# Two transformer-like blocks on one core: more seven-product slots in the second feed-forward products, and three of four of their weight sums made during the first products, kept in DRAM and loaded

## The chip, the cores and the metric

The kernel runs on 1 core of one Trainium2 chip. The metric is the device time of a launch in microseconds (us). The kernel before took a median of 2221.39 us over 3 runs (2220.28 to 2221.83).

## The reference

Two blocks on 256 tokens of width 2048 in fp32, one after the other. Each has a mixer (block 1: neighbourhood attention, a state-space mixer and memory attention; block 2: four kinds of attention) and a feed-forward part. What matters here is the feed-forward part, width 8192, twice in the program:

```python
h = rmsnorm(x, norm_mlp_pre[l])
f = jnp.square(jax.nn.relu(h @ w_ff1[l])) @ w_ff2[l]     # block 1; block 2: w_up, w_down
x = x + rmsnorm(f, norm_mlp_post[l])
```

## The kernel before

**Precision.** Products of fp32 matrices are made of three matmuls on rounded parts: high x high, high x low, low x high. For each weight tile ScalarE writes the rounded high part and VectorE the low part (tile minus high). TensorE can only start on a slot when both have passed over it.

**Slots.** Weights come through a ring of 4 slots of 1 MB (128 partitions x 2048 floats, `raw_weights`), loaded by the queue of SyncE (SP): it waits on `split_ready` until VectorE has split the slot four earlier, then asks for the next load. High and low parts (`w_high`, `w_low`) have two buffers each. Every engine walks the slots in the order in which the program writes them out, and engines meet by semaphores.

**Ups.** `up` makes the hidden layer (`ff1_1` of block 1, `ff1_2` of block 2): 8 iterations of 8 slots. A slot is 16 wide matmuls (512 columns) and 16 narrow ones (256). After slots 0 and 4 of an iteration ScalarE and VectorE move a finished group out of PSUM (`evac_hidden`, `summed`, `squared`). The order on VectorE is `low(0)`, `low(1)`, `summed`, `squared`, `low(2)` and so on, where `low(j)` splits slot j.

**Downs.** `down` multiplies the hidden layer by the second weights (`ff2_1`, `ff2_2`): two passes h = 0, 1 over the left and right 1024 output columns, each 32 slots r of 2 x 128 rows. A **plain slot** is 4 banks x 2 row tiles x 3 = 24 matmuls of 512 columns (lines 841 to 843). A **seven-product slot** (the list `SUMMED`, 11 of the 32) takes its 2 x 2 blocks of weights W0..W3 and of activations by Strassen's scheme in Winograd's form: 7 block products instead of 8, so 21 matmuls (lines 856 to 858). For this it needs sums. `sums(h, r)` on VectorE makes, in this order, s1 and s3 of x, the weight sums t1 and t3 (W1 + W0, W2 + W0; 128 x 1024, L2603), s2, t2 = W2 + t1 (L2607), s4, and t4 = W3 + t2, which overwrites W0 in the ring (L2611). Then ScalarE rounds and VectorE splits: the four plain blocks as `quad_high` and `quad_low` (L1709, L2619), the sums of x (L2617, L2621) and t1, t3, t2 (L2623, L2625). All these have one buffer. ScalarE rounds `quad_high` when TensorE has done the first four products of the seven-product slot before (`quad_used`), and the other sums when it has done that slot (`split_used`).

**The order on VectorE.** `down` goes over r: first `sums` of slot r + 1 if that is a seven-product slot, then the split of slot r itself. The first sums of a pass stand ahead of slot 0, those of slot 2 of the first pass in a scratch of their own. In the first pass `last_summed` and `last_squared` of the up stand behind slots 0 and 1. Four `keep` steps stand about slot 0 of the second pass, and `combine` (the seven products' banks into `home`) ahead of slot 30. In the last pass of `ff2_2` there are also two left halves (L2390), ahead of slots 29 and 30, and two `ahead` steps (L2397), ahead of slot 31. TensorE there does banks 0 to 2 of slots 30 and 31 before bank 3 of both.

GpSimd has no part in the ups and downs, and issues no DMA.

## Time and profile before

| | |
|---|---|
| median of 3 runs | 2221.39 us |
| the profiled execution, span | 2219.3 us |
| TensorE busy | 2195.5 us, 99% |
| VectorE busy | 1613.8 us, 73% |
| ScalarE busy | 1163.2 us, 52% |
| GpSimd busy | 93.2 us, 4% |
| DMA, mean rate | 181 GB/s |
| granted TensorE clock, mean | 0.999 |
| first up, first down | about 426 to 785 us, 785 to 1119 us |
| second up, second down | about 1510 to 1873 us, 1873 to 2206 us |

A timeline row has the start, the length, the engine, the line, the operation, its output and inputs, and in brackets the idle time before it with what ended it. Lengths of neighbouring operations overlap, since an engine starts one while the last drains: the price of an operation is the distance between two starts. A row with x2 holds two operations merged.

### The profile page before, as it was taken

How to read it: one execution, taken by the hardware profiler on the slowest of the kernel's cores; microseconds unless marked ns; L12 is line 12 of the kernel's file. 1: busy time of each engine (PE TensorE's matmuls, PEld its weight loads, DVE VectorE, ACT ScalarE, POOL GpSimd, SP SyncE). 2: the span in 40 equal slices, each digit the busy share in tenths (PEclk: the TensorE clock that was granted, in tenths of full speed). 3: DMA queues.
4: the chain of work that ended last, by engine and by line, in shares of the span. 5: the costliest groups of instructions: out<-in, count | busy, mean ns of one | idle time of the engine just before them, and what ended most of it. 6: DMA issues, size and time to landing. Idle time of an engine off the chain costs nothing.

```text
span 2219.3 us, 32872 instructions
## 1 busy us (share of the span) xinstructions
PE 2195.5 (99%) x13128; PEld 1892.6 (85%) x13128; DVE 1613.8 (73%) x2013; ACT 1163.2 (52%) x1682; POOL 93.2 (4%) x66
## 2 busy tenths in 40 slices
PE   8999999999999999999999999999999999999998
PEld 7888988888888888888898988888888888888886
DVE  7878565665454599899886578847454547998997
ACT  6433465543443466566664466646434345665665
POOL 0553000000000000000000000000000000000000
PEclk9999999999999999999999999999999999999999
DMA  8364445555556666667654533455565565666663
GB/s 328 121 153 161 151 134 211 168 190 189 189 188 188 187 194 207 195 205 258 199 166 144 172 115 98 136 196 163 187 189 189 189 189 173 215 201 195 209 202 114
DMA packets 169923, 402.65 MB, mean 181 GB/s; under 512 B 15296, under 2 KB 30912, under 8 KB 165968
## 3 DMA queue, kind: packets, MB, share of 16 engines
q1 hardware_dynamic: 158496, 394.83, 55.3%
q10 hardware_dynamic: 11312, 6.22, 1.2%
q8 instruction: 80, 1.31, 0.2%
q14 instruction: 35, 0.29, 0.0%
HBM read 398.90 MB, written 2.13 MB: 181 GB/s over the span
## 4 chain that ended last, share of the span: by engine, by line
PE 94%; DVE 4%; ACT 1%; issue 1%; DMA 0%; SPq 0%; DVEq 0%; ACTq 0%
PE ps L768 21%; PE ps L773 11%; PE ps L841 7%; PE ps L842 6%; PE ps L843 6%; PE ps L657 5%; PE ps L857 3%; PE ps L856 3%; PE ps L858 3%; PE ps L665 3%; PE ps L666 3%; PE ps L667 3%; PE ps L1075 2%; PE ps L1077 2%; PE ps L1076 2%; PE ps L679 2%
## 5 line engine op out<-in xcount | busy, mean ns | idle before, releaser
L2497 DVE TENSOR_TENSOR w_low<-raw_weights,w_high 128x1024 fp32r<-128x1024 f32 (+1 forms) x403 | 474.3, 1215 | 422.1 <-ACT w_high L1574 418.3
L1574 ACT ACTIVATE w_high<-raw_weights 128x1024 fp32r<-128x1024 f32 (+1 forms) x378 | 377.4, 1046 | 408.0 <-PE ps L773 279.8
L768 PE MATMUL ps<-x_split,w_high 128*128 128x512 f32 x2048 | 494.1, 391 | 1.7 <-DVE x_split L2485 1.7
L768 PEld LDWEIGHTS ps<-x_split,w_high 128*128 128x128 f32 x2048 | 374.6, 188 | 74.2 <-issue 3.0
L773 PEld LDWEIGHTS ps<-x_split,w_low 128*128 128x128 f32 x2048 | 265.8, 191 | 12.1
L773 PE MATMUL ps<-x_split,w_low 128*128 128x256 f32 x2048 | 269.4, 283 | 0.0
L841 PE MATMUL ps<-w_high,x_split 128*128 128x512 f32 x672 | 262.0, 390 | 0.5 <-issue 0.4
L842 PE MATMUL ps<-w_low,x_split 128*128 128x512 f32 x672 | 261.5, 389 | 0.0
L843 PE MATMUL ps<-w_high,x_split 128*128 128x512 f32 x672 | 261.4, 389 | 0.0
L2582 DVE TENSOR_TENSOR w_low<-raw_weights,w_high 128x1024 fp32r<-128x1024 f32 x168 | 197.8, 1219 | 1.7 <-ACT w_high L1689 1.6
L1689 ACT ACTIVATE w_high<-raw_weights 128x1024 fp32r<-128x1024 f32 x168 | 167.6, 1045 | 0.0
L666 PE MATMUL ps<-x_split,w_high 128*128 128x256 f32 x544 | 153.8, 283 | 0.0
L841 PEld LDWEIGHTS ps<-w_high,x_split 128*128 128x128 f32 x672 | 126.1, 188 | 29.0 <-issue 3.0
L843 PEld LDWEIGHTS ps<-w_high,x_split 128*128 128x128 f32 x672 | 126.1, 188 | 26.3
L842 PEld LDWEIGHTS ps<-w_low,x_split 128*128 128x128 f32 x672 | 126.2, 188 | 25.7
L665 PE MATMUL ps<-x_split,w_high 128*128 128x256 f32 x416 | 121.4, 292 | 0.8 <-DVE x_split L2485 0.4
L667 PE MATMUL ps<-x_split,w_low 128*128 128x256 f32 x416 | 117.5, 282 | 0.0
L657 PE MATMUL ps<-x_over_high,raw_weights 128*128 128x256 f32 x512 | 115.0, 382 | 0.0
L1709 ACT ACTIVATE x_split<-raw_weights 128x1024 fp32r<-128x1024 f32 x88 | 88.1, 1048 | 47.1 <-DVE raw_weights L2611 47.1
L2619 DVE TENSOR_TENSOR x_split<-raw_weights,x_split 128x2048 fp32r<-128x2048 f32 x44 | 100.7, 2288 | 16.2 <-ACT x_split L1709 16.2
L657 PEld LDWEIGHTS ps<-x_over_high,raw_weights 128*128 128x128 f32 x512 | 95.9, 190 | 14.6 <-issue 1.2
L666 PEld LDWEIGHTS ps<-x_split,w_high 128*128 128x128 f32 x544 | 104.2, 191 | 0.2
(376 smaller groups left out, 3657.9 us busy)
## 6 DMA issues: line engine op xcount, KB each, us to landing
raw_weights<-in_w_ff SPq DMA_DIRECT2D x128, 1024.0 KB, 5.4
raw_weights<-in_w_up SPq DMA_DIRECT2D x64, 1024.0 KB, 5.2
raw_weights<-in_w_down SPq DMA_DIRECT2D x64, 1024.0 KB, 5.5
raw_weights<-in_w_in SPq DMA_DIRECT2D x62, 1024.0 KB, 5.3
raw_weights<-in_w_out SPq DMA_DIRECT2D x32, 1024.0 KB, 4.9
raw_weights<-in_w_mem_kv SPq DMA_DIRECT2D x7, 1024.0 KB, 14.6
residual<-in_xT SPq DMA_DIRECT2D x2, 2048.0 KB, 13.9
region<-t_table ACTq DMA_DIRECT2D x1, 3072.0 KB, 18.9
```

The lines of the kernel that those rows point to most:

```text
L657: last = nc.tensor.matmul(acc[:, c], w[:, P * c:P * c + P], x, start=(kt == 0 and c % 2 == 0), stop=(kt == kts - 1), skip_group_check=True)
L665: nc.tensor.matmul(o, h, xh_, start=(first and c % 2 == 0), stop=False, skip_group_check=True)
L666: nc.tensor.matmul(o, h, xl_, start=False, stop=False, skip_group_check=True)
L667: last = nc.tensor.matmul(o, wl[:, P * c:P * c + P], xh_, start=False, stop=done, skip_group_check=True)
L768: nc.tensor.matmul(hidden_ps(g)[:, c], w[:, P * c:P * c + P], xs[:, kt], start=(kt == 0), stop=False, skip_group_check=True)
L773: last = nc.tensor.matmul(hidden_ps(g)[:, c, 0:S], w[:, P * c:P * c + P], xh[:, kt], start=False, stop=(kt == KT - 1), skip_group_check=True)
L841: nc.tensor.matmul(o, x_high[:, x], wh[:, c], start=(r == 0 and q == 0), stop=False, skip_group_check=True)
L842: nc.tensor.matmul(o, x_high[:, x], wl[:, c], start=False, stop=False, skip_group_check=True)
L843: last = nc.tensor.matmul(o, x_low[:, x], wh[:, c], start=False, stop=True, skip_group_check=True)
L1574: nc.scalar.activation(split_slot(wh_t, k)[:, r], ring_slot(n)[:, r], ACT.Copy).then_inc(rounded, 1)
L2497: V.tensor_tensor(split_slot(wl_t, k)[:, r], ring_slot(n)[:, r], split_slot(wh_t, k)[:, r].bitcast(f32), ALU.subtract).then_inc(split_read ...
L2582: V.tensor_tensor(split_slot(wl_t, k)[:, w], ring_slot(n)[:, w], split_slot(wh_t, k)[:, w].bitcast(f32), ALU.subtract).then_inc(split_read ...
```

## The change

Seven-product slots are now 2, 4, ... 28, so 14 a pass instead of 11. Counted through both passes of a down (0 to 27), all but every fourth (3, 7, ... 27) are **staged**: 21 a down. During the up before it, GpSimd loads the 1 MB of weights of such a slot into a free tile (`mix_t` or `xres_t`), VectorE makes t1, t3, t2 and t4 in three additions after slots 0, 3 and 6 of each iteration but the first, and GpSimd stores the four sums as a record in DRAM, with the load of the next record beside it. In the down SP loads t1, t3 and t2 straight to where ScalarE rounds them, and t4 in the place of W0, beside W1 and W2, W3, into the ring slot, by three DMAs; `sums` makes only the sums of x. The first record's load waits for `t5_masked` in `ff1_1` and for `residual_row` 1 in `ff1_2`. SP's queue in the down is unrolled, and at its slot 4 waits for the last record and the end of the up. The sums of slot 2 now stand between slots 0 and 1 in both passes, and `combine` ahead of slot 31. On ScalarE `first_product` moves one slot later as well. The diff, cut to its core:

```diff
+        w_sums = nc.dram_tensor("weight_sums", (28, P, 2048), f32, kind="Internal").ap()
...
-        sums_at = [(rinv, place("sums", 22528, 1024)), (region[:, 16384:17408], region[:, 17408:18432])]
+        sums_a, sums_b = rinv, place("sums", 22528, 1024)
+        stage_of = {"ff1_1": mix_t, "ff1_2": xres_t, "ff2_1": mix_t, "ff2_2": xres_t}
...
-        SUMMED = (2, 5, 7, 10, 12, 15, 17, 20, 22, 25, 27)
+        SUMMED = tuple(range(2, PAIRS - 3, 2))
+        AHEAD_OF = tuple(j for j in range(2 * len(SUMMED)) if j % 4 != 3)
+        RECORDS = len(AHEAD_OF)
+        STAGED = RECORDS // (FF1_ITERS - 1)
+        STAGE0 = {"ff1_1": 0, "ff1_2": RECORDS, "ff2_1": 0, "ff2_2": RECORDS}
...
+        def ahead_count(name, c):
+            return STAGE0[name] + sum(j < c for j in AHEAD_OF)
+        def made_before(name, c):
+            return 6 * (SUMMED0[name] + c) - 3 * ahead_count(name, c)
...
             def down(name, w):
-                for j in range(BODY):
-                    load(rows(w, 0, 1024, 2 * j, 2))
                 n0, k0 = SLOT0[name], SPLIT0[name]
-                for lo, hi, back, c0 in ((1, FF2_ITERS // 2, 0, 0), (FF2_ITERS // 2, FF2_ITERS, DFF, 1024)):
-                    with sp.Fori(lo, hi) as i:
-                        for j in range(BODY):
-                            sp.wait_ge(split_ready, i * (2 * BODY) + 2 * (k0 + j - RING + 1))
-                            src = w[bass.ds(i * (2 * BODY * P) + (2 * P * j - back), 2 * P), c0:c0 + 1024]
-                            sp.dma_start(ring_slot(n0 + j).rearrange("p (k c) -> p k c", k=2),
-                                         src.rearrange("(k p) c -> p k c", p=P)).then_inc(slot_loaded[(n0 + j) % RING], 16)
-                state["n"] = n0 + BODY * FF2_ITERS
+                before = {}
+                for c in AHEAD_OF:
+                    before[4 if c == 0 else slot_before(c - 1, SUMMED) + 4] = c
+                for q in range(2 * PAIRS):
+                    (h, r), n = divmod(q, PAIRS), n0 + q
+                    sp.wait_ge(split_ready, 2 * (k0 + q - RING + 1))
+                    if q == 4:
+                        sp.wait_ge(staged, 32 * (STAGE0[name] + RECORDS))
+                        sp.wait_ge(split_used, k0)
+                    if q in before:
+                        c = before[q]
+                        sp.dma_start(sums_a, w_sums[AHEAD_OF.index(c), :, 0:1024]).then_inc(raws_loaded, 16)
+                        sp.dma_start(sums_b[:, 0:512], w_sums[AHEAD_OF.index(c), :, 1024:1536]).then_inc(raws_loaded, 16)
+                    if r in SUMMED and summed_count(h, r) in AHEAD_OF:
+                        c = summed_count(h, r)
+                        got = rest_loaded[ahead_count(name, c) % 2]
+                        src = w[2 * P * r:2 * P * (r + 1), 1024 * h:1024 * h + 1024].rearrange("(k p) c -> p k c", p=P)
+                        sp.dma_start(ring_slot(n)[:, HALF:SLOT], src[:, 1]).then_inc(slot_loaded[n % RING], 16)
+                        sp.dma_start(ring_slot(n)[:, 512:HALF], src[:, 0, 512:1024]).then_inc(got, 16)
+                        sp.dma_start(ring_slot(n)[:, 0:512], w_sums[AHEAD_OF.index(c), :, 1536:2048]).then_inc(got, 16)
+                    else:
+                        src = w[2 * P * r:2 * P * (r + 1), 1024 * h:1024 * h + 1024].rearrange("(k p) c -> p k c", p=P)
+                        sp.dma_start(ring_slot(n).rearrange("p (k c) -> p k c", k=2), src).then_inc(slot_loaded[n % RING], 16)
+                state["n"] = n0 + 2 * PAIRS
...
                     act.wait_ge(split_used, SPLIT0[name])
+                    act.wait_ge(staged, 32 * (STAGE0[name] + RECORDS))
                 act.wait_ge(gains_loaded, 16)
                 nc.scalar.activation(sh[:, 0:384], pair_of(r, P, 384), ACT.Copy).then_inc(sums_rounded, 1)
                 act.wait_ge(slot_loaded[n % RING], 16 * (n // RING + 1))
-                act.wait_ge(sums_made, 6 * s + 6)
+                if c in AHEAD_OF:
+                    u = ahead_count(name, c)
+                    act.wait_ge(rest_loaded[u % 2], 32 * (u // 2 + 1))
+                else:
+                    act.wait_ge(sums_made, made_before(name, c + 1))
                 for half_ in range(2):
                     a = slice(SLOT // 2 * half_, SLOT // 2 * (half_ + 1))
                     nc.scalar.activation(quad_high[:, a], w[:, a], ACT.Copy).then_inc(rounded, 1)
                 if c:
                     act.wait_ge(split_used, SPLIT0[name] + slot_before(c - 1, SUMMED) + 1)
+                act.wait_ge(sums_made, made_before(name, c + 1))
                 nc.scalar.activation(sh[:, 384:896], sums_b[:, 512:1024], ACT.Copy).then_inc(sums_rounded, 1)
+                if c in AHEAD_OF:
+                    act.wait_ge(raws_loaded, 32 * (ahead_count(name, c) + 1))
                 nc.scalar.activation(th[:, 0:1024], sums_a, ACT.Copy).then_inc(sums_rounded, 1)
...
-                        if r == PAIRS - 3:
+                        if r == PAIRS - 2:
                             first_product(name, h + 1)
...
+            def stage(name, w, free):
+                t = stage_of[name]
+                def store(c):
+                    pool.wait_ge(sums_staged, ADDS * (STAGE0[name] + c + 1))
+                    if c + 1 < RECORDS:
+                        load(c + 1)
+                    pool.dma_start(w_sums[c], t[:, 2048:4096]).then_inc(staged, 16)
+                def load(c):
+                    h, r = AHEAD_OF[c] // len(SUMMED), SUMMED[AHEAD_OF[c] % len(SUMMED)]
+                    src = w[2 * P * r:2 * P * (r + 1), 1024 * h:1024 * h + 1024].rearrange("(k p) c -> p k c", p=P)
+                    pool.dma_start(t[:, 0:2048].rearrange("p (k c) -> p k c", k=2), src).then_inc(staged, 16)
+                free()
+                load(0)
+                for c in range(RECORDS):
+                    store(c)
...
+            stage("ff1_1", A["w_ff2"], lambda: pool.wait_ge(dve_done, at("t5_masked")))
...
+            stage("ff1_2", A["w_down_2"], lambda: pool.wait_ge(act_done, at("residual_row", 1)))
...
+                t = stage_of[name]
+                w, sums_ = (t[:, a:a + 2048].rearrange("p (b c) -> p b c", c=512) for a in (0, 2048))
+                stage_after = {0: 0, 3: 1, 6: 2}
+                def staged_sums(q, i):
+                    c = STAGE0[name] + q - STAGED
+                    dve.wait_ge(staged, i * (32 * STAGED) + (32 * c + 16))
+                    V.tensor_tensor(sums_[:, 0:2], w[:, 1:3], w[:, 0].unsqueeze(1).to_broadcast([P, 2, 512]), ALU.add).then_inc(sums_staged, 1)
+                    dve.wait_ge(sums_staged, i * (3 * STAGED) + (3 * c + 1))
+                    V.tensor_tensor(sums_[:, 2], w[:, 2], sums_[:, 0], ALU.add).then_inc(sums_staged, 1)
+                    dve.wait_ge(sums_staged, i * (3 * STAGED) + (3 * c + 2))
+                    V.tensor_tensor(sums_[:, 3], w[:, 3], sums_[:, 2], ALU.add).then_inc(sums_staged, 1)
                 def body(i, first=False):
                     for j in range(4 if first else 0, BODY):
                         low(name, j, i)
+                        if j in stage_after and not first:
+                            staged_sums(stage_after[j], i)
...
                 def sums(h, r):
-                    n, s = SLOT0[name] + PAIRS * h + r, SUMMED0[name] + summed_count(h, r)
-                    (sums_a, sums_b), w = scratch_of(h, r), ring_slot(n).rearrange("p (b c) -> p b c", c=512)
-                    t1, t2, t13 = sums_a[:, 0:512], sums_b[:, 0:512], sums_a.rearrange("p (b c) -> p b c", c=512)
+                    n, s, c = SLOT0[name] + PAIRS * h + r, SUMMED0[name] + summed_count(h, r), summed_count(h, r)
                     s1, s2, s4 = sums_b[:, 512:640], sums_b[:, 768:896], sums_b[:, 896:1024]
                     s13 = sums_b[:, 512:768].rearrange("p (b c) -> p b c", c=P)
                     x = pair_of(r).rearrange("p (b c) -> p b c", c=P)
                     if h == 0:
                         dve.wait_ge(hidden_ready, HIDDEN_OF[name] + r // 2 + 1)
-                    if (h, r) == (0, SUMMED[0]):
-                        dve.wait_ge(t5_out, 16)
-                    elif (h, r) == (0, SUMMED[1]):
-                        dve.wait_ge(split_used, SPLIT0[name])
-                    c = summed_count(h, r)
                     if c:
                         dve.wait_ge(split_ready, 2 * (SPLIT0[name] + slot_before(c - 1, SUMMED) + 1))
+                    else:
+                        dve.wait_ge(split_used, SPLIT0[name])
                     V.tensor_tensor(s13, x[:, 0:2], x[:, 2::-2], ALU.subtract).then_inc(sums_made, 1)
+                    m0 = made_before(name, c)
+                    if c in AHEAD_OF:
+                        dve.wait_ge(sums_made, m0 + 1)
+                        V.tensor_tensor(s2, s1, x[:, 1], ALU.subtract).then_inc(sums_made, 1)
+                        dve.wait_ge(sums_made, m0 + 2)
+                        V.tensor_tensor(s4, x[:, 3], s2, ALU.add).then_inc(sums_made, 1)
+                        return
...
-                        if r == PAIRS - 2:
+                        if r == PAIRS - 1:
                             combine(name, h + 1)
                         if (h, r) == (1, PAIRS - 1) and ahead is not None:
                             for t in range(TT):
                                 ahead(t)
-                        if r == 0:
-                            sums(h, SUMMED[0])
-                            if h:
-                                keep(name, 0)
-                        elif r + 1 in SUMMED[1:]:
+                        if (h, r) == (1, 0):
+                            keep(name, 0)
+                        if r + 1 in SUMMED:
                             sums(h, r + 1)
                         if r in SUMMED:
                             summed(h, r)
```

## Rows read from the trace of the kernel before

**Rows 1.** The page: the span, and busy time, share and count of each engine.

```profile
span 2219.3 us, 32872 instructions
...
PE 2195.5 (99%) x13128; PEld 1892.6 (85%) x13128; DVE 1613.8 (73%) x2013; ACT 1163.2 (52%) x1682; POOL 93.2 (4%) x66
```

**Rows 2.** Windows, an up, a down: stretch, length, busy time by engine, clock, DMA.

```profile
560.00:700.00 140.00, 140.00 (x805) 123.69 (x805) 72.49 (x63) 56.65 (x57) 0.00 (x0) 1.00 0.59 188
...
850.00:1000.00 150.00, 149.65 (x661) 123.61 (x660) 139.67 (x174) 91.57 (x117) 0.00 (x0) 1.00 0.64 203
```

**Rows 3.** Timeline, TensorE, a down: start, length, engine, line, operation, tiles.

```profile
905.00 0.39 PE L841 MATMUL ps<-w_high,x_split 128*128 128x512 f32 x1
...
915.88 0.39 PE L856 MATMUL ps<-x_split,mem_high 128*128 128x512 f32 x1
...
920.64 0.39 PE L841 MATMUL ps<-w_high,x_split 128*128 128x512 f32 x1
```

**Rows 4.** Timeline, VectorE, a down: six sums, then a plain slot.

```profile
902.89 0.41 DVE L2601 TENSOR_TENSOR sums<-region 128x256 f32<-128x256 f32 x1
...
903.23 1.22 DVE L2603 TENSOR_TENSOR rinv<-raw_weights 128x1024 f32<-128x1024 f32 x1
...
904.36 0.28 DVE L2605 TENSOR_TENSOR sums<-sums,region 128x128 f32<-128x128 f32 x1
...
905.97 0.69 DVE L2578 TENSOR_TENSOR x_split<-region,x_split 128x512 fp32r<-128x512 f32 x1
...
908.84 0.55 DVE L2617 TENSOR_TENSOR mem_high<-region,mem_high 128x384 fp32r<-128x384 f32 x1
```

**Rows 5.** Timeline, ScalarE: it rounds a seven-product slot.

```profile
919.28 1.99 ACT L1709 ACTIVATE x_split<-raw_weights 128x1024 fp32r<-128x1024 f32 x2
```

**Rows 6.** Timeline, VectorE: it splits that slot, and what comes next.

```profile
921.31 2.29 DVE L2619 TENSOR_TENSOR x_split<-raw_weights,x_split 128x2048 fp32r<-128x2048 f32 x1 [0.75 <-ACT x_split L1709]
...
925.86 0.68 DVE L2578 TENSOR_TENSOR x_split<-region,x_split 128x512 fp32r<-128x512 f32 x1
```

**Rows 7.** Timeline, VectorE: the operation behind plain slot 1, first down.

```profile
790.81 1.22 DVE L2544 SCALAR_TENSOR_TENSOR region<-region 128x1024 f32<-128x1024 f32 x1
```

**Rows 8.** Timeline, TensorE: it begins plain slot 1 of the first down.

```profile
791.04 0.47 PE L841 MATMUL ps<-w_high,x_split 128*128 128x512 f32 x1
```

**Rows 9.** Timeline, TensorE: it begins the last slot of the kernel.

```profile
2200.02 0.47 PE L841 MATMUL ps<-w_high,x_split 128*128 128x512 f32 x1
```

**Rows 10.** Timeline, VectorE, the end of the second down.

```profile
2186.80 1.28 DVE L2390 SCALAR_TENSOR_TENSOR region<-region,small_stats,mixed 128x1024 f32<-128x1024 f32 x1
...
2188.88 1.41 DVE L2261 TENSOR_TENSOR region<-region,ps 128x512 f32<-128x512 f32 x2 [0.80 <-ACT region L1723]
...
2194.40 2.60 DVE L2397 SCALAR_TENSOR_TENSOR region<-region,small_stats,mixed 128x1024 f32<-128x1024 f32 x2
...
2197.52 2.35 DVE L2582 TENSOR_TENSOR w_low<-raw_weights,w_high 128x1024 fp32r<-128x1024 f32 x2
```

**Rows 11.** Timeline, VectorE, an up: splits of slots, idle before each.

```profile
625.40 2.36 DVE L2497 TENSOR_TENSOR w_low<-raw_weights,w_high 128x1024 fp32r<-128x1024 f32 x2 [3.20 <-ACT w_high L1574]
...
631.96 2.36 DVE L2497 TENSOR_TENSOR w_low<-raw_weights,w_high 128x1024 fp32r<-128x1024 f32 x2 [4.20 <-ACT w_high L1574]
```

**Rows 12.** Timeline, TensorE, an up: two slots begin.

```profile
629.67 3.82 PE L768 MATMUL ps<-x_split,w_high 128*128 128x512 f32 x16
...
635.24 3.82 PE L768 MATMUL ps<-x_split,w_high 128*128 128x512 f32 x16
```

**Rows 13.** DMA view, 12 to 45 us: packets, rate, many in flight.

```profile
DMA packets 4924, 13.13 MB, mean 398 GB/s; under 512 B 351, under 2 KB 479, under 8 KB 4538
```

**Rows 14.** DMA view, 560 to 700 us: issues, size, median us to landing.

```profile
raw_weights<-in_w_ff SPq DMA_DIRECT2D x25, 1024.0 KB, 5.2
```

**Rows 15.** Timeline, VectorE, first up: the t5 mask, then slot 1.

```profile
468.31 0.68 DVE L2261 TENSOR_TENSOR region<-ps,region 16x512 f32<-16x512 f32 x1 [0.47 <-PE ps L748]
...
476.12 2.36 DVE L2497 TENSOR_TENSOR w_low<-raw_weights,w_high 128x1024 fp32r<-128x1024 f32 x2 [4.86 <-ACT w_high L1574]
```

More of the change, by code:

```diff
@@ L275, in program @@
         out_written = sem("out_written")
+        staged, sums_staged = sem("staged"), sem("sums_staged")
+        rest_loaded, raws_loaded = [sem(f"rest{i}_loaded") for i in range(2)], sem("raw_sums_loaded")
         block = ctx.enter_context(nc.Block())
@@ L479, in pair_of @@
             return hid_f[:, 512 * r + a:512 * r + a + width]
-        def scratch_of(h, r):
-            return sums_at[1 if (h, r) == (0, SUMMED[0]) else 0]
         def ring_slot(n):
@@ L1694, in summed @@
                 s, w = SUMMED0[name] + c, ring_slot(n)
-                sums_a, sums_b = scratch_of(h, r)
                 th, sh = sums_w[name][0], sums_x[name][0]
```

12 lines of the change are left out of this document (7 added, 5 removed).

## The prediction

> **What bounds the kernel now.** I read the page's table of busy times first. TensorE is busy for 99% of the span [rows 1]: a change gains only by taking matmuls away, and loses wherever TensorE is made to wait. The profiled execution took 2219.3 us; the median of the runs is 2221.39, so about 2.1 us lie around the span, and I add the sum of this text to the median. Next, the busy times by stretch [rows 2]: in an up VectorE works 72.5 of 140 us, in a down 139.7 of 150. That share hides the order of the work, so I then read both engines slot by slot. In the down a plain slot is 24 matmuls and a seven-product slot 21, and TensorE goes from slot to slot without a gap [rows 3]: (915.88 - 905.00) / 48 = 0.2267 us for each matmul, 5.44 us for a plain slot, (920.64 - 915.88) = 4.76 for a seven-product slot.
>
> **Term 1, matmuls.** SUMMED grows from 11 to 14 slots in each of four passes: 12 more slots, 3 matmuls fewer in each, 36 x 0.2267 = 8.2 us less. This is certain as work.
>
> **Term 2, the seven-product slot that still makes its own sums (14 times).** On VectorE the six sums take 905.97 - 902.89 = 3.08 us, and the split of a plain slot behind them 908.84 - 905.97 = 2.87 [rows 4]. For a staged slot only the three small sums of x remain, 0.41 + 0.28 + 0.28 with waits between them, about 1.0. So VectorE's total falls, by 42 x 2.1 us. Its place counts more. How soon can VectorE have a seven-product slot ready when the last one but one was also such a slot? The splits have one buffer: ScalarE's rounding waits for TensorE's four first products, VectorE's split of them for the rounding, and the rest for the end of that earlier slot. The trace has this spacing: TensorE ends the earlier slot at 920.64 [rows 3], ScalarE had begun to round at 919.28 [rows 5], VectorE waited for it, split at 921.31 and was free for the next thing at 925.86 [rows 6], 5.2 us after TensorE's end. Before, every such pair was followed by two plain slots, and the six sums of the next one came only after the first of these had been split. After, all seven-product slots stand two apart (2, 4, ... 28), and `sums(h, r + 1)` stands directly ahead of the plain split that TensorE needs next. From TensorE's end of a seven-product slot: 5.2 + 3.08 + 2.87, with about 0.15 for the semaphore, is 11.3; TensorE wants it after one plain and one seven-product slot, at 5.44 + 4.76 = 10.2. It waits 1.1 us. With a staged slot: 5.2 + 1.0 + 2.87 + 0.15 = 9.2, no wait. Of counts 0 to 27 every fourth (3, 7, ... 27) is unstaged, 7 in each down; the one early in the second pass starts with a little less on VectorE (I take 0.9). 2 x (6 x 1.1 + 0.9) = 15 us. The wait cannot be made up: VectorE may not run ahead of the single buffer, however idle it is on average. This term is larger than the gain.
>
> **Term 3, the ends of the downs.** Up to down: VectorE is done with plain slot 1 at 790.81 [rows 7] and TensorE begins it at 791.04 [rows 8], 0.2 us to spare. Before, the first sums were made ahead of slot 0, into a scratch of their own; now about 1.0 us of small sums stands between: 0.8 to 0.9 late, twice, 1.8. First to second pass: the last `keep` ends some 0.9 after TensorE's end of slot 31 (it reads its bank), then 1.0 + 2.87 and the semaphore against 5.44: 0.4 late, twice, 0.8. End of the kernel: after slot 27 VectorE had four plain slots, two left halves, `combine` and two `ahead` steps, and was late for slot 31 by a little (the split of slot 31 runs from 2197.52 to 2199.87 [rows 10] and TensorE begins it at 2200.02 [rows 9]; in step it would have begun some 0.3 earlier). Now slot 28 is a seven-product slot; behind it come 3 x 2.87 for plain slots, 2 x 1.28 for left halves, two pairs of 1.4 for `combine` (about 2.7) and 2.5 for `ahead`, 16.4 us [rows 4, 10], beginning 5.0 us before TensorE's end of it, thus some 11.3 after; TensorE wants slot 31 after 24 + 18 matmuls, 9.5. With the semaphore that is 1.6 to 1.9 late instead of 0.3: 1.4. Together 4.0 us.
>
> **Term 4, the ups.** The three sums per record cost 1.22 [rows 4] + 0.68 + 0.68 (an operation of 128 x 512 [rows 6]) = 2.6 us on VectorE, 42 times, 109 us. They stand where VectorE waits 3.2 us a slot, 4.2 once [rows 11]: hidden, with 0.6 us to spare. TensorE needs 5.57 us a slot (635.24 - 629.67 [rows 12]). What isn't sure is the wait for the record's DMAs, `staged`, with all of VectorE's splits queued behind it, and TensorE behind them. A load and a store of 1 MB go out from GpSimd when the sums are made. The shortest of the three intervals is two slots: 11.1 - 2.6 = 8.5 us until VectorE asks, and TensorE feels it 2.5 later (1.6 that VectorE would idle, 0.9 by which its split is ahead, 634.3 [rows 11] against 635.24 [rows 12]): 11.0. The 16 DMA engines together moved 398 GB/s when all were wanted [rows 13], and one 1 MB load takes 5.2 us to land [rows 14]: 2.6 us are its 1.05 MB at that rate, and 2.6 are fixed. A pair that shares the engines with one ring load: 2.6 + 3 x 2.6 = 10.5, just inside. Over an iteration the need is 14 x 1.05 MB in 44.5 us, 330 GB/s, 83% of the 398. The trace has neither a store of this size nor a GpSimd DMA, so the ends are: 0, and three transfers one behind the other at 5.2, 15.6 - 11.0 = 4.6 us at each of 12 places, 55 us. I take 0, by the nearer row (398 with many in flight), and keep half of the upper end for the range. Nothing below 0: no matmul is removed here. The first load of `ff1_1` goes out only after `t5_masked` (468.31 + 0.68 [rows 15]) and lands 5.2 later, 474.2, or 475.2 with some time for the issue; sums to 477.8, where VectorE went on to slot 1 at 476.12 [rows 15]: 1.7 late against 0.9 of lead, 1 us. In `ff1_2` the load goes out earlier: 0.
>
> The 5.2 us [rows 14] belong to SP's loads. The Trainium skill, "DMA: Bandwidth & Descriptors", section "Issuing engines are not separate DMA queues", says that DMAs issued from GpSimd run on the same 16 engines as those of SP; it speaks against this change, since it gives the stage's traffic no path of its own. Its table of transfers issued from GpSimd has 6.15 us for 1 MB; by that figure a pair in line would take 12.3 and each of the 12 places cost an estimated 1.3 us, 16 us in all. No row here shows such a transfer.
>
> **Edits costed at nothing.** Each staged slot brings 0.75 MB more in the down: 10.75 MB in 40.8 us, 263 GB/s of 398; the raw sums are asked for when the slot before is split and needed some 10 us later, against 5.2. SP waits at slot 4 for the end of the up and for `staged`; queued behind it is slot 4's load, needed three slots (15 us) later. The t5 table (3 MB, second pass of the first down) shares this time: 0 to 3 us. ScalarE's new waits are for landings of the same kind, and it idles beside TensorE. The unrolled SP queue: it only issues.
>
> **Sum.** -8.2 + 15 + 4.0 + 1 = +11.8, and about 1 for the t5 overlap and small delays: 2234.
>
> **Rivals.** (1) The own sums hide after all: TensorE gets its 8.2 us, only terms 3 and half of 4 stay, 2221.4 - 8.2 + 4 = 2217; without term 3 too, 2213. It decides if VectorE is free within 10.2 - 3.08 - 2.87 - 0.15 = 4.1 us of TensorE's end instead of 5.2. For it: VectorE is 93% busy in the down before [rows 2] and would do less, and no wait of this kind stands in the trace; against it: the 5.2 us are a row, and the order is in the code. 0.10. (2) The own sums cost half, 0.5 us each, if VectorE is ready sooner than in the row: 2227. 0.12. (3) The ups wait for `staged`: from a landing later than 11.0 us after the sums each us costs 12; 1 to 2 us (an issue on GpSimd, the receipt of a store) on top of the forecast give 2246 to 2258. For it: a margin of 0.5 us against unmeasured parts. 0.24. (4) The engines saturate below 330 GB/s when loads and stores mix: 14.7 MB at 300 is 48.9 us instead of 44.5, 14 times 4.4, 2296. Loads alone reached 398. 0.05. (5) The change doesn't save what it says: excluded for the matmuls, whose slots are counted in the code. The forecast, 2229 to 2240, has 0.49.
>
> **The range.** Rival 4 and most of rival 1 are left out: 2219 to 2257. A measurement of this kernel can tell 0.2%, 4.4 us, from no change. Faster, below 2217: half of rival 1 and less, 0.06. Within: the rest of it and a part of rival 2, 0.10. Slower: 0.84.
>
> **What the profile of after would show.** 2 x 2 x (18 x 24 + 14 x 21) = 2904 matmuls in the downs, at 0.2267. Waits of TensorE of about 1.1 us before the plain slots 7, 15, 23 of the first passes and 3, 11, 19, 27 of the second, released by VectorE's w_low; none before the plain slots ahead of staged ones. The first plain slot after an up 0.9 late. In the ups, waits of VectorE for `staged` below 2.5 us, and no gap of TensorE; if TensorE has gaps at the second slot of each iteration, rival 3 is right. I'm wrong altogether if VectorE finishes a seven-product slot much sooner than 5.2 us after TensorE's end of the one before.

## The result

The kernel after takes 2245.53 us (median of 4 runs, 2242.28 to 2249.43), the kernel before 2221.61 in the same comparison: a ratio of 1.011, 95% interval 1.0096 to 1.0123. It is 24 us slower, where 12.4 were forecast. Of the runs below, one execution of six of spread_sync took 2415.45 us at a granted clock of 0.849 where the others had 0.998 to 0.999, and is left out of its median.

The profile's page of after: span, then engines with busy time, share and count; below, queues with packets, MB and share of the 16 engines, and two kinds of transfers with count, size and us to landing.

```profile
span 2247.6 us, 33030 instructions
...
PE 2198.2 (98%) x13092; PEld 1890.4 (84%) x13092; DVE 1695.2 (75%) x2109; ACT 1182.4 (53%) x1718; POOL 146.7 (7%) x150
...
q1 hardware_dynamic: 177312, 427.87, 55.9%
q0 software_dynamic: 17472, 88.09, 12.1%
...
mixed<-in_w_ff POOLq DMA_DIRECT2D x21, 1024.0 KB, 7.5
weight_sums<-mixed POOLq DMA_DIRECT2D x21, 1024.0 KB, 9.8
```

Windows of after, an up and a down, with the columns of [rows 2]:

```profile
560.00:700.00 140.00, 137.61 (x786) 121.06 (x786) 94.93 (x89) 55.79 (x56) 11.38 (x18) 1.00 0.94 324
850.00:1000.00 150.00, 146.66 (x644) 120.24 (x643) 131.49 (x163) 94.23 (x124) 0.00 (x0) 1.00 0.73 246
```

Against [rows 1], 36 matmuls are gone, as wanted, yet the span is 28.3 us longer. Against [rows 2], VectorE does less in the down (131.5 us for 139.7), and TensorE loses 3 us there all the same; in the up it loses 2.4, beside transfers at 324 GB/s instead of 188. TensorE's waits in after: engine, line, what it waited for; us in all, times, longest.

```profile
PE ps L868 <- DVE w_low L2654: 20.0, 19, 2.1
...
PE ps L795 <- DVE w_low L2553: 6.6, 5, 2.0
```

Line 868 is the first product of a plain slot, line 795 that of an up's slot. I call a gap what lies between the starts of two matmuls beyond the usual 0.23 us; these are the gaps of after, by kind. **Own sums:** in each down slots 7, 15 and 23 of the first pass begin 1.39 us late, slots 3, 11, 19 and 27 of the second 0.76, 1.27, 1.27, 1.27, one of these 1.27 being 2.26 in the first down: 18.5 us. **Ends:** slot 1 after each up 1.02, slot 1 of each second pass 0.43, the last slot 1.63: 4.5. Before had 0.8 at such places, 0.31 at its last slot and 0.52 at the start of one second pass, so 3.7 are new. **Ups:** 1.94, 1.58, 0.91, 0.34 and 2.04: 6.8. Three stretches of TensorE at half clock, below, cost some 5. With -8.2 for the matmuls the sum is 26; about 2.5 of the profiled 28.3 us I can't place, and this execution was the slowest of the four.

VectorE in after, about slot 7 of the first down, answers [rows 4] and [rows 6]:

```profile
819.10 2.29 DVE L2694 TENSOR_TENSOR x_split<-raw_weights,x_split 128x2048 fp32r<-128x2048 f32 x1 [1.09 <-ACT x_split L1740]
...
823.83 0.42 DVE L2668 TENSOR_TENSOR sums<-region 128x256 f32<-128x256 f32 x1
824.17 1.22 DVE L2679 TENSOR_TENSOR rinv<-raw_weights 128x1024 f32<-128x1024 f32 x1
...
826.92 0.69 DVE L2650 TENSOR_TENSOR x_split<-region,x_split 128x512 fp32r<-128x512 f32 x1
827.52 2.36 DVE L2654 TENSOR_TENSOR w_low<-raw_weights,w_high 128x1024 fp32r<-128x1024 f32 x2
829.79 0.56 DVE L2692 TENSOR_TENSOR mem_high<-region,mem_high 128x384 fp32r<-128x384 f32 x1
```

And TensorE behind it:

```profile
830.02 0.47 PE L868 MATMUL ps<-w_high,x_split 128*128 128x512 f32 x1 [1.23 <-DVE w_low L2654]
```

In step TensorE would have begun at 830.02 - 1.39 = 828.63, so it had ended the seven-product slot before at 818.43. VectorE was free 5.4 us later, the sums took 3.09, the split 2.87, the semaphore 0.23: 11.6 against 10.2. That the 5.4 us come from the single buffer is read from the order in the code and from VectorE's wait for ScalarE (1.09 us at 819.10); no run gives it a second buffer.

### The profile page after: what moved, and what is told of

It reads as the page before. It is cut to its first block, busy times and chain, and to the rows that moved or that the text cites. A ratio compares the mean times of both kernels' runs of the same rounds, so it can differ in the third digit from the quotient of the medians.

```text
span 2247.6 us, 33030 instructions
## 1 busy us (share of the span) xinstructions
PE 2198.2 (98%) x13092; PEld 1890.4 (84%) x13092; DVE 1695.2 (75%) x2109; ACT 1182.4 (53%) x1718; POOL 146.7 (7%) x150
## 4 chain that ended last, share of the span: by engine, by line
PE 77%; DVE 13%; issue 3%; ACT 3%; DMA 3%; POOL 0%; DVEq 0%; SPq 0%; ACTq 0%
PE ps L795 17%; PE ps L800 9%; PE ps L684 5%; PE ps L868 4%; PE ps L869 4%; PE ps L870 4%; PE ps L692 3%; PE ps L693 3%; PE ps L694 3%; PE ps L1102 2%; PE ps L1103 2%; PE ps L1104 2%; DVE w_low L2654 2%; PE ps L885 2%; PE ps L883 2%
## 5 line engine op out<-in xcount | busy, mean ns | idle before, releaser
L868 PE MATMUL ps<-w_high,x_split 128*128 128x512 f32 x576 | 226.5, 393 | 20.0 <-DVE w_low L2654 20.0
L870 PE MATMUL ps<-w_high,x_split 128*128 128x512 f32 x576 | 224.9, 390 | 0.0
L869 PE MATMUL ps<-w_low,x_split 128*128 128x512 f32 x576 | 224.8, 390 | 0.0
L2654 DVE TENSOR_TENSOR w_low<-raw_weights,w_high 128x1024 fp32r<-128x1024 f32 x144 | 169.6, 1220 | 1.5 <-ACT w_high L1716 1.5
L2694 DVE TENSOR_TENSOR x_split<-raw_weights,x_split 128x2048 fp32r<-128x2048 f32 x56 | 128.3, 2292 | 43.0 <-ACT x_split L1740 43.0
L868 PEld LDWEIGHTS ps<-w_high,x_split 128*128 128x128 f32 x576 | 108.5, 188 | 49.5 <-issue 27.4
L1716 ACT ACTIVATE w_high<-raw_weights 128x1024 fp32r<-128x1024 f32 x144 | 143.8, 1047 | 0.0
L870 PEld LDWEIGHTS ps<-w_high,x_split 128*128 128x128 f32 x576 | 108.5, 188 | 22.9
L869 PEld LDWEIGHTS ps<-w_low,x_split 128*128 128x128 f32 x576 | 108.6, 189 | 21.9
L1740 ACT ACTIVATE x_split<-raw_weights 128x1024 fp32r<-128x1024 f32 x112 | 111.7, 1046 | 0.6 <-DVE raw_weights L2687 0.6
```

The costliest lines, as they stand in the source:

```text
L868: nc.tensor.matmul(o, x_high[:, x], wh[:, c], start=(r == 0 and q == 0), stop=False, skip_group_check=True)
L869: nc.tensor.matmul(o, x_high[:, x], wl[:, c], start=False, stop=False, skip_group_check=True)
L870: last = nc.tensor.matmul(o, x_low[:, x], wh[:, c], start=False, stop=True, skip_group_check=True)
L2654: V.tensor_tensor(split_slot(wl_t, k)[:, w], ring_slot(n)[:, w], split_slot(wh_t, k)[:, w].bitcast(f32), ALU.subtract).then_inc(split_read ...
```

## Experiments

All times are medians; before stood at 2220.8 to 2221.0 in these comparisons. **First the two halves of the loss, each by itself.**

**own_out.** The three weight additions of an unstaged slot are left out (its products are then of stale sums).

```diff
-                    V.tensor_tensor(t13, w[:, 1:3], w[:, 0].unsqueeze(1).to_broadcast([P, 2, 512]), ALU.add).then_inc(sums_made, 1)
...
-                    V.tensor_tensor(t2, w[:, 2], t1, ALU.add).then_inc(sums_made, 1)
...
-                    V.tensor_tensor(s4, x[:, 3], s2, ALU.add).then_inc(sums_made, 1)
-                    dve.wait_ge(sums_made, m0 + 4)
-                    V.tensor_tensor(w[:, 0], w[:, 3], t2, ALU.add).then_inc(sums_made, 1)
+                    V.tensor_tensor(s4, x[:, 3], s2, ALU.add).then_inc(sums_made, 4)
```

> The kernel after without the three weight additions of the seven-product slots that are not staged (it leaves out these sums, 14 times in the run, so its products there are wrong; the sums of x stay). If VectorE's own sums ahead of the plain slot's split are what TensorE waits for, the 14 gaps of 1.1 to 1.5 us ahead of plain slots 7, 15, 23 (first half) and 3, 11, 19, 27 (second) go, 18.5 us in all: about 2227 us, against 2245.5 with them. If the ups' transfers or the later loads cost the time, it stays within 3 us of 2245.

Measured 2225.11 us, ratio to before 1.0018 (1.0009 to 1.0027). Additions of 14 x 2.3 = 33 us of VectorE's time are gone (1.14 + 0.60 + 0.60 by the starts in the rows above and around them), and the kernel gains 20.4. No plain slot waits inside a pass any more; the gaps at the ends and in the ups are left, the one at the last slot with 2.12 us instead of 1.63.

**staging_only.** The kernel before, with the staging added to the ups.

```diff
+            stage("ff1_1", A["w_ff2"], lambda: pool.wait_ge(dve_done, at("t5_masked")))
...
+            stage("ff1_2", A["w_down_2"], lambda: pool.wait_ge(act_done, at("residual_row", 1)))
...
                         low(name, j, i)
+                        if j in stage_after and not first:
+                            staged_sums(stage_after[j], i)
```

> The kernel before with the staging of the ups alone: 21 loads, additions and stores in each up, into a tensor that nothing reads; the downs make all their sums as before. If the ups' stalls (6.8 us of gaps in the trace of after) and the stretch at the lower clock behind one of them (1.7 us) come from the staging, 2228 to 2232 us against 2221.6. If the staging is hidden, as the forecast took it but for 1 us, 2222 to 2224. If VectorE's own sums are the whole loss, also 2222 to 2224.

Measured 2230.14, ratio 1.0041 (1.0028 to 1.0054): 9.3 us, for work that the forecast had nearly hidden. One gap in its second up is 6.3 us long:

```profile
1843.10 2.50 PE L775 MATMUL ps<-x_split,w_high 128*128 128x512 f32 x5 [6.23 <-DVE w_low L2527]
```

VectorE's wait before it, and GpSimd's issue before that:

```profile
1838.09 1.23 DVE L2584 TENSOR_TENSOR residual<-residual 128x1024 f32<-128x1024 f32 x1 [8.86 <-DMA weight_sums<-residual]
```

```profile
1829.59 0.58 POOL L2259 DMA_DIRECT2D weight_sums<-residual  x1 [7.83 <-issue]
```

The sums had long been made and GpSimd waited for nothing that the profile shows; yet the store went out 7.8 us late. The additions can't overwrite `sums_` before it has landed, and every split is queued behind them. In all nine kernels in which GpSimd issues 84 transfers (after among them) it is the 79th that is held so, for 5.6 to 8.7 us. Its release follows the transfer before it, the 78th, a load that took 7.3 us from its issue to its landing:

```profile
1821.07 0.70 POOL L2264 DMA_DIRECT2D residual<-in_w_down  x1 [15.53 <-DVE residual L2588]
...
residual<-in_w_down POOLq DMA_DIRECT2D x1, 1024.0 KB, 7.3
```

It landed at 1828.37, 1.22 us before the held issue, and that distance is 1.22 in all nine kernels. The two runs add up: -8.2 + 20.4 + 9.3 + 3.7 (ends) = 25.2, against 24 measured.

**Then the order of VectorE's work.** split_first makes the own sums behind the plain slot's split; halves adds a second edit on ScalarE; spread puts the first weight addition back in front. All three leave the staging as it is. The edit of split_first:

```diff
+                        own = r + 1 in SUMMED and summed_count(h, r + 1) not in AHEAD_OF
-                        if r + 1 in SUMMED:
+                        if r + 1 in SUMMED and not own:
                             sums(h, r + 1)
...
                             plain(h, r)
+                        if own:
+                            sums(h, r + 1)
```

> The kernel after, with the sums that are not staged made behind the plain slot's split in VectorE's order instead of ahead of it. If their place is the cause, the 1.3 us gaps ahead of the plain slots go and smaller ones come ahead of the seven-product slots, whose rounding on ScalarE then starts later: 2236 to 2241 us. If the length of the chain is the cause wherever it stands, 2244 to 2247, with the gaps one slot later.

Measured 2250.10, ratio 1.0132 (1.0117 to 1.0147): worse by 4.6, a miss for both. VectorE at the first own slot of the first down:

```profile
826.75 0.69 DVE L2687 TENSOR_TENSOR raw_weights<-raw_weights,sums 128x512 f32<-128x512 f32 x1
827.35 0.56 DVE L2692 TENSOR_TENSOR mem_high<-region,mem_high 128x384 fp32r<-128x384 f32 x1
829.58 2.29 DVE L2694 TENSOR_TENSOR x_split<-raw_weights,x_split 128x2048 fp32r<-128x2048 f32 x1 [1.67 <-ACT x_split L1740]
...
835.91 2.35 DVE L2654 TENSOR_TENSOR w_low<-raw_weights,w_high 128x1024 fp32r<-128x1024 f32 x2
```

VectorE ends the sums at 827.4, then stands 1.67 us while ScalarE rounds, because ScalarE couldn't begin before the last sum. TensorE pays twice, 0.7 ahead of the seven-product slot and 0.95 ahead of the plain slot behind it, instead of 1.3 once. In after this rounding ran beside the plain slot's split.

halves, on ScalarE:

```diff
-                else:
-                    act.wait_ge(sums_made, made_before(name, c + 1))
-                for half_ in range(2):
+                for half_ in (range(2) if c in AHEAD_OF else (1, 0)):
+                    if c not in AHEAD_OF and half_ == 0:
+                        act.wait_ge(sums_made, made_before(name, c + 1))
```

> split_first, and ScalarE rounds the half of a slot that needs no sum first (W2 and W3), where it otherwise waits for all sums before both halves. If the wait for the sums ahead of the first half is what the reordered kernel still pays, another 6 to 10 us go: 2228 to 2234 us. If ScalarE's own work (3 us a slot behind the sums) sets it, the time stays at that of split_first.

Measured 2236.04, ratio 1.0069 (1.0057 to 1.0081): the first gap is gone but for one of 0.27, 0.7 to 0.9 ahead of the plain slot behind are left (0.2 at the first of a second pass). It is 14 us below split_first, 2 above the range: the step was larger than expected, and began higher.

spread, on VectorE, against halves (part 0 is s1, s3, t1, t3; part 1 the rest):

```diff
+                        if own:
+                            sums(h, r + 1, 0)
...
                             plain(h, r)
                         if own:
-                            sums(h, r + 1)
+                            sums(h, r + 1, 1)
```

> halves, with the first weight addition of a slot that is not staged (W1 and W2 plus W0, 1.2 us) back ahead of the plain slot's split, and the other two behind it. If a chain that is short on both sides is what counts, the gaps of 0.7 to 0.9 us that halves has left behind each such slot go, 10 us in all: 2226 to 2230 us, with own_out (2225.1) as the floor. If every addition costs its share wherever it stands, 2234 to 2238, as halves.

Measured 2237.19, ratio 1.007 (1.0057 to 1.0084): no gain over halves, as its second branch had it. The gap stays at 0.8 to 1.0. In the orders tried, with slots two apart throughout, an own set costs 0.7 to 1.65 us (1.3 in after), less at the first of a second pass. In before an own set ahead of a single plain slot costs nothing (slots 12, 17, 22 and 27) or 0.2 us (slot 7): there the seven-product slot before it has two plain slots ahead of itself.

**fourteen_own.** The kernel before with 14 seven-product slots a pass and no staging; `combine` and `first_product` stand one slot later, as in after.

```diff
-        SUMMED = (2, 5, 7, 10, 12, 15, 17, 20, 22, 25, 27)
+        SUMMED = tuple(range(2, PAIRS - 3, 2))
```

> The kernel before with seven-product slots at 2, 4, to 28 as in after, 28 in a down, all their sums made by VectorE during the downs and nothing staged. Per group of four slots VectorE then makes two sets of weight sums: 5.3 us more a group, twice after's half. If VectorE's chain ahead of a plain slot costs 1.3 us wherever a set is made, 56 sets less the 8.2 us of matmuls: 2280 to 2295 us. If only VectorE's total counted (94% busy), 2225 to 2235.

Measured 2265.20, ratio 1.0195 (1.0181 to 1.0209): between the two, a miss for both. Its waits, and its window of a down:

```profile
PE ps L841 <- DVE w_low L2582: 37.4, 52, 1.9
```

```profile
850.00:1000.00 150.00, 143.65 (x623) 115.80 (x622) 145.19 (x186) 88.38 (x117) 0.00 (x0) 1.00 0.62 194
```

VectorE is busy for 145.2 of 150 us, 97%, and hardly waits (0.5 us in the first 100): it is now the bound, and each pair of slots takes 0.8 us more than TensorE's 10.2. So there are two limits, VectorE's total (0.8 a pair when every set is own) and its chain behind a single buffer (1.3 when one in four is). Staging does help at this spacing: 2265.2 to 2245.5.

**eleven.** After with before's slots, 21 of the 22 of a down staged.

```diff
-        SUMMED = tuple(range(2, PAIRS - 3, 2))
+        SUMMED = (2, 5, 7, 10, 12, 15, 17, 20, 22, 25, 27)
-        AHEAD_OF = tuple(j for j in range(2 * len(SUMMED)) if j % 4 != 3)
+        AHEAD_OF = tuple(range(2 * len(SUMMED) - 1))
```

> The kernel after with the seven-product slots of before (2, 5, 7, to 27), 21 of the 22 of a down staged. The matmuls are before's, no plain slot of a down but one in each has a whole set of sums ahead of it, and every seven-product slot has two or three slots between it and the next. If the staging costs what it cost alone, 2228 to 2231 us; with less work for VectorE in the downs, the ends may give 1 to 2 us back. If the loads of the sums delay the downs, 2233 or more.

Measured 2233.86, ratio 1.0056 (1.0043 to 1.0069). That is the range for delayed downs, but its trace has no gap inside a pass, so the loads of sums delay nothing there. The ends, which I had expected to give 1 to 2 us, took 5.8: 1.0 twice, 0.4 twice, and 2.95 at the last slot, where `combine` stands directly ahead of the split. With the lower clock behind that last gap they more than cover the 3 us above the first range.

**The ups.** store_first:

```diff
+                    pool.dma_start(w_sums[c], t[:, 2048:4096]).then_inc(staged, 16)
                     if c + 1 < RECORDS:
                         load(c + 1)
-                    pool.dma_start(w_sums[c], t[:, 2048:4096]).then_inc(staged, 16)
...
-            stage("ff1_1", A["w_ff2"], lambda: pool.wait_ge(dve_done, at("t5_masked")))
+            stage("ff1_1", A["w_ff2"], lambda: pool.wait_ge(dve_done, at("mlp", "folded")))
```

> The kernel after, where GpSimd issues the store of a record ahead of the load of the next one, and the first load of the first up waits for the folded squares (464 us in the trace) instead of the table's mask (469.5). If the ups' stalls hang on the store's late start, the 1.9 us gap at 482 us goes, VectorE's waits for the store (15.7 and 14.2 us in all) halve, and the ups give back 4 to 6 us: 2239 to 2242 us against 2245.5. In five kernels the 79th transfer that GpSimd issues was held for 6.5 to 7.8 us; it was a store. If it is the count that matters, the 79th is held here too, and is a load. If the ups' stalls come from the rate of the transfers alone, the time stays at 2244 to 2247.

Measured 2245.69, ratio 1.0109 (1.0093 to 1.0124): nothing gained, though this is also where the forecast put a stall by the rate alone. The gap at 482 is gone, but others of 0.9 to 2.7 us have come (in the trace of its slowest execution, 5.7 us above the median), and VectorE waits for loads instead of stores:

```profile
DVE mixed L2610 <- DMA mixed<-in_w_ff: 20.7, 7, 4.5
DVE residual L2610 <- DMA residual<-in_w_down: 20.5, 7, 5.3
```

The 79th transfer of GpSimd is held again, and here it is a load:

```profile
1837.62 0.57 POOL L2283 DMA_DIRECT2D weight_sums<-residual  x1 [15.53 <-DVE residual L2614]
1844.47 0.71 POOL L2290 DMA_DIRECT2D residual<-in_w_down  x1 [6.28 <-issue]
```

**best** is named for what was hoped of it: spread and store_first, the sums of x for slot 2 behind the split of slot 1, and the last `combine` and `ahead` steps behind the split of slot 31.

```diff
-                        if (h, r) == (1, PAIRS - 1) and ahead is not None:
...
                             plain(h, r)
...
+                        if (h, r) == (0, 1):
+                            sums(h, r + 1)
+                        if end:
+                            combine(name, h + 1)
+                            for t in range(TT):
+                                ahead(t)
```

> spread and store_first together, the sums of x for slot 2 behind the split of slot 1 at the start of each down (two gaps of 1.0 us), and the last combination of products behind the split of the last slot (the gap of 1.6 to 2.6 us ten microseconds before the end). From spread: 2.0 and 2.1 us less at these places, 4 to 6 us less in the ups: 2218 to 2223 us, level with the kernel before (2220.9) or 0.1% faster. If spread gives nothing over halves: 2226 to 2230.

Measured 2242.18, ratio 1.0096 (1.0081 to 1.0112): a miss by 20 us. The gap at slot 1 moved to slot 3 (0.88), the gap at the last slot went, and two of 1.9 and 2.1 took its place before the final transposes. One of 1.1 stands there in spread, so the step behind the last split gave nothing. That best is 5 us slower than spread is not explained: the profiled execution of spread was its slowest, 7.3 us above its median, with a gap of 7.1 us behind the held 79th issue, so the two traces can't be compared for it.

**sync_first and spread_sync** hand the staged transfers to SyncE, which issues them behind its weight loads at slots 4, 7 and 2, as soon as the additions are made. The first load of the first up waits for the folded squares, as in store_first.

```diff
+                            if j == 2 and i > 1:
+                                stage_store(STAGED * (i - 1) - 1)
+                            if j in (4, 7):
+                                stage_store(STAGED * (i - 1) + (j == 7))
```

(`stage_store` waits for `sums_staged` and issues the next record's load and this one's store.)

> The kernel after, with the 42 staged transfers of the first up issued by SyncE behind its weight loads, and those of the second up by GpSimd as in after. If it is the count of GpSimd's transfers that holds the 79th (6.3 to 8.7 us in seven kernels), no issue of GpSimd is held any more, as it has only 42, and the gaps late in the second up (2 us and the lower clock behind) go: about 2241 us against 2245.5. If it is the place in the second up, its 37th transfer is held again: 2243 to 2246. If two queues at once are what slows the transfers, the first up is 4 us shorter too: 2237 to 2240.

Measured 2238.65, ratio 1.0081 (1.0068 to 1.0094): 6.9 us less, with one up of two changed. GpSimd in the second up, its 36th and 37th transfer there (the 37th is the one that was the 79th):

```profile
1829.42 0.70 POOL L2327 DMA_DIRECT2D residual<-in_w_down  x1 [15.53 <-DVE residual L2650]
1830.11 0.57 POOL L2322 DMA_DIRECT2D weight_sums<-residual  x1
```

No issue is held, and the second up has 0.3 us of gaps instead of 2.4: it is the count, not the place. The first up, too, has no gap over 0.1 us inside, where after had 4.4, but its end has a new one of 1.84. That puts the time in the lowest of the three ranges.

> spread, with all 84 staged transfers issued by SyncE behind its weight loads. If GpSimd's queue (its late issue, its own stream beside the weights) makes the ups' stalls, 5 to 8 us less than spread (2237.2): 2229 to 2232 us. If the rate of the transfers makes them, they stay, as waits for the weights' loads: 2236 to 2240.

Measured 2231.81, ratio 1.0052 (1.0039 to 1.0065): 5.4 less than spread, in the range. Neither up has a gap, but each down begins 1.7 to 1.8 late: SyncE waits for the last sums before it asks for the down's first slot. The rate did not fall: 330 GB/s in the window 560 to 700 us, as with GpSimd (324 in after, 332 in spread). So it was not the rate of the 16 engines alone that stalled the ups.

Nor did single transfers land sooner: in twelve, below, which stages the same way, a load takes 7.6 us and a store 9.6 in the first up. What did change is the way to the issue. VectorE's last addition and SyncE's two issues in twelve:

```profile
579.94 0.69 DVE L2650 TENSOR_TENSOR mixed<-mixed 128x512 f32<-128x512 f32 x1
...
580.65 0.37 SPq L548 DMA_DIRECT2D mixed<-in_w_ff  x1
581.07 0.47 SPq L554 DMA_DIRECT2D weight_sums<-mixed  x1
```

The store goes out 0.44 us after the additions' end (580.63), in after 0.99 us. That is half a us of a limit that the pairs of after passed by 0.4 to 2.1, as term 4 below shows; the slowest pairs also took less long, and why is not shown. The queue, the moment of issue and the earlier first load changed together; they were not separated.

**twelve** puts together what was learned: slots three apart where a set is own, SyncE's queue, the last store behind the first loads of the down, the ends as before. Its slots, against after:

```diff
-        SUMMED = tuple(range(2, PAIRS - 3, 2))
-        AHEAD_OF = tuple(j for j in range(2 * len(SUMMED)) if j % 4 != 3)
+        SUMMED = (2, 5, 7, 9, 12, 14, 16, 19, 21, 23, 25, 27)
+        AHEAD_OF = tuple(j for j in range(2 * len(SUMMED)) if j not in (4, 7, 16))
```

> What the runs so far point to, in one kernel: twelve seven-product slots a pass (2, 5, 7, 9, 12, 14, 16, 19, 21, 23, 25, 27), 21 of the 24 of a down staged, the three others at places with two plain slots ahead of them and their sums as in spread; all staged transfers issued by SyncE, the last store behind the first loads of the down; the ends of a pass as in before, and the first sums of x behind the split of slot 1. Against before: 4 more seven-product slots, 12 matmuls of 0.2267 us less (2.7 us); 0.3 to 1 us of gaps in the ups, up to 2 us at the starts of the downs. If the spacing and GpSimd's queue were the causes, 2218 to 2222 us: level with before (2221.0), 0.1% faster at best. If VectorE's sums or the sums' loads cost time wherever they stand, 2226 or more.

Measured 2218.24 against 2220.84, ratio 0.9987 (0.9978 to 0.9996), in the range. Its page, and the same two windows:

```profile
span 2216.4 us, 32590 instructions
...
PE 2193.1 (99%) x13116; PEld 1891.3 (85%) x13116; DVE 1652.5 (75%) x2045; ACT 1168.1 (53%) x1694; POOL 93.1 (4%) x66
```

```profile
560.00:700.00 140.00, 140.00 (x805) 123.71 (x804) 97.89 (x93) 56.53 (x57) 0.00 (x0) 1.00 0.95 331
850.00:1000.00 150.00, 149.73 (x661) 123.73 (x660) 124.93 (x151) 93.95 (x122) 0.00 (x0) 1.00 0.73 254
```

12 matmuls fewer than before are worth 2.7 us, and 2.6 came. The up moves 331 GB/s and TensorE is busy for all of it, as in [rows 2]. The downs have three gaps left, 0.43, 0.43 and 0.31, of which the profile counts two as waits:

```profile
PE ps L906 <- DVE w_low L2690: 0.5, 2, 0.3
```

It is the only kernel here that beats before, by 0.12% of the medians; the interval lies just below 1, and the gain is less than the 0.2% that the forecast took for the limit.

## Why the forecast was right, and where not

The sign and the largest term were right; the point was low by 11.5 us. The measured 2245.5 lies above the forecast's 2229 to 2240, at the lower edge of rival 3 (2246 to 2258), and inside the range only because that was kept wide. By its steps:

- **Term 1**, -8.2 us: 13128 - 13092 = 36 matmuls, as counted. twelve shows that each is worth its 0.2267 us.
- **Term 2**, 15 us: the wait and all 14 places were right, the sizes 1.39 and 1.27 instead of 1.1 (0.76 for 0.9). VectorE was free 5.4 us after TensorE's end, not 5.2, and the semaphore took 0.23, not 0.15: that is the 0.3. One place was 1 us dearer: ScalarE waited for the raw sums beside the t5 table, and the lower clock behind it cost 1.7 more. The trace has 18.5 us of gaps; without the additions the kernel takes 20.4 less. As a rule for other spacings the working doesn't hold: fourteen_own, forecast by it, came out 15 us below its range.

```profile
1054.40 1.06 ACT L1747 ACTIVATE mem_high<-rinv 128x1024 fp32r<-128x1024 f32 x1 [1.81 <-DMA sums<-weight_sums]
```

- **Term 3**, 4.0 us: slot 1 after the ups 1.02 for 0.9, slot 1 of the second passes 0.43 for 0.4, the last slot 1.63 for 1.6 to 1.9. Right, against [rows 7, 8, 9].
- **Term 4**, 1 us, is the step that failed: 9.3 measured. Its first load was seen (VectorE waits 5.20 us, TensorE 1.9):

```profile
476.95 1.23 DVE L2610 TENSOR_TENSOR mixed<-mixed 128x1024 f32<-128x1024 f32 x1 [5.20 <-DMA mixed<-in_w_ff]
```

  The rest was taken as 0 because a pair was to land within 10.5 us of the sums, where 11.0 was the limit. The limit was right and the landing was not. Beside each other a load took 7.5 us and a store 9.8, ring loads 7.3 to 7.9 instead of the 5.2 of [rows 14], and GpSimd needed 0.7 us for the first issue before it came to the second. The pair behind slot 6 that stalls at 573 us: the last addition, GpSimd's two issues, VectorE's wait for the store, TensorE's.

```profile
554.70 0.69 DVE L2614 TENSOR_TENSOR mixed<-mixed 128x512 f32<-128x512 f32 x1
...
555.68 0.70 POOL L2290 DMA_DIRECT2D mixed<-in_w_ff  x1 [15.53 <-DVE mixed L2614]
556.38 0.57 POOL L2285 DMA_DIRECT2D weight_sums<-mixed  x1
...
568.01 1.23 DVE L2610 TENSOR_TENSOR mixed<-mixed 128x1024 f32<-128x1024 f32 x1 [4.17 <-DMA weight_sums<-mixed]
...
573.01 0.74 PE L795 MATMUL ps<-x_split,w_high 128*128 128x512 f32 x2 [1.53 <-DVE w_low L2553]
```

  From the end of the additions (555.39) to the landing it is 12.6 us, and 12.6 - 11.0 is the gap of 1.6. Of the 12 such pairs four in after took more than 11.0, 11.4, 11.9, 12.6 and 13.1 (this one held), and TensorE waited 0.34, 0.91, 1.58 and 2.04 us; the others took 9.9 to 11.0. In twelve they took 9.0 to 10.5, and nothing waited. Rival 3 had named this (1 to 2 us late at 12 places, 0.24); it happened at four. VectorE's waits for `staged`, forecast below 2.5 us, reached 4.6 behind a pair. The held 79th issue was in no row of before, and the lower clock behind a gap wasn't costed.
- **The range** doesn't follow from its own rule: half of the upper end of term 4 is 27.5 us, which would put the top at 2261, not 2257. Nothing turned on it.
- The Trainium skill, "DMA: Bandwidth & Descriptors", section "Issuing engines are not separate DMA queues", says that GpSimd's transfers share the 16 engines. By that rule the ring's loads should slow down beside them, and the trace agrees: 5.2 us before, 7.9 after in the same window. Its table's 6.15 us is for a 1 MB load alone, without the making of its descriptors; from issue to landing beside the other loads 7.5 were measured here. The estimate of 16 us for the ups that the prediction made from it stands against 9.3 measured.
- **Rivals 1 and 2** fell with own_out: the own sums hide nowhere. **Rival 4**, saturation below 330 GB/s, fell with twelve, which moves 331 without a gap.

## What to carry to other kernels

A busy share doesn't say whether the steps that stay are in time: here an own set cost 0.7 to 1.65 us where seven-product slots stood two apart throughout, with VectorE 88% busy, and 0.2 or nothing in before and in twelve, where two plain slots came often enough in between. Hidden transfers need a landing time measured in the mix, counted from the end of the work that releases them, with margin to spare: here pairs of 10.5 us cost nothing and one of 11.4 did. Before giving up on a rate, try another queue, since the same 330 GB/s cost 9 us in one way and nothing in another (twelve). When `SUMMED`'s last slot moves, read the end of the pass slot by slot: small steps there cost 4 us.

## What the hardware showed besides

**A held issue.** In each of nine kernels with 84 transfers issued by GpSimd the 79th was issued 5.6 to 8.7 us late, whether it was a load or a store; with 42 none was. It goes out 1.22 us after the landing of the 78th in all nine, as if the queue had to run empty first; no other issue of GpSimd's in these kernels waits so. GpSimd's queue had moved 16352 packets by then where the 79th is a store, 16224 where it is a load. Whether such a count sets it, no run tests; the queue that carries instructions had no transfer near it.

**TensorE's clock.** The granted clock fell from 2.4 to 1.2 GHz for 3.4 us three times in after: just behind the gaps of 2.3 us at 1063.9 and 2.0 us at 1852.15, and once at 1395.6 in work that the change doesn't touch. Windows of after, in the low stretch and a few us on:

```profile
1853.00:1856.40 3.40, 3.40 (x10) 2.63 (x9) 3.37 (x4) 0.00 (x0) 0.00 (x0) 0.51 0.89 278
1860.00:1863.40 3.40, 3.40 (x18) 2.84 (x17) 2.66 (x3) 1.66 (x2) 0.00 (x0) 1.00 1.05 402
```

10 matmuls instead of 18: some 1.7 us each time. At the gaps of 6.3 and 7.1 us in staging_only and spread the clock was low for 6.8 us, but it fell inside the gap, and only 3.3 and 4.6 us of it lay behind. Not every shorter gap has it: those of 1.94 us at 482 in after and 2.11 at 2206 in own_out had none, and of 22 gaps of 1.8 to 3.0 us in the ups and downs of all traces 10 were followed by it. So a gap near 2 us may cost almost twice its length. Whether that is behind the spread between runs of one kernel (7 us in after, 1.5 in twelve) is not shown.
